# Starting two units of an output line beside the last attention tiles (second of three transformer blocks)

## The reference, cut to what matters

```
h = rmsnorm(x, attn_norm);  proj = h @ w_in
o_nsa  = head_rmsnorm(nsa_mixer(p_nsa),  nsa_out_gain)     # 6 heads of 64: features 0..383
o_rw   = rwkv7_mixer(p_rw)                                 # 4 heads of 64: features 384..639
o_moba = head_rmsnorm(moba_mixer(p_moba), moba_out_gain)   # 6 heads of 64: features 640..1023
x = x + concatenate([o_nsa, o_rw, o_moba]) @ w_out
x = x + conv_glu(rmsnorm(x, ffn_norm), ...)
```

## Time and profile before

| | us |
|---|---|
| median of three timed runs | 2748.77 |
| the three runs | 2742.35, 2748.77, 2754.93 |
| profiled execution, its own time | 2737.73 |
| its span, first to last instruction | 2735.6 |
| TensorE busy in it | 2610.8 (95%) |
| mean granted TensorE clock | 0.978 of full |

### The profile page before, as it was taken

The page is one execution under the profiler, slowest core; times in us unless marked ns, Lnnn a source line. Parts: engine busy times, 40 slices in busy tenths (PEclk is TensorE's granted clock), DMA queues, the critical chain, the costliest instruction groups (busy, mean ns, idle before and its releaser), DMA issues.

```text
span 2735.6 us, 35675 instructions
## 1 busy us (share of the span) xinstructions
PE 2610.8 (95%) x14346; PEld 2114.1 (77%) x14346; DVE 1514.5 (55%) x2530; ACT 1036.0 (38%) x1821; POOL 320.1 (12%) x263
## 2 busy tenths in 40 slices
PE   8989999999999999998989999999999999999998
PEld 6778888899998876766657777777766677788886
DVE  4787654554445456477646778454643544433444
ACT  3465444443223252235443223254333333322323
POOL 0043310012222010010002222020000000100001
PEclk9999999999999999998789999999999999999999
DMA  3211121223222331320024564232221122233332
GB/s 131 71 50 55 47 63 63 70 86 92 93 93 86 99 132 47 123 70 2 1 70 146 200 200 154 94 115 85 78 70 47 54 85 89 84 97 93 94 99 69
DMA packets 70849, 239.00 MB, mean 87 GB/s; under 512 B 12212, under 2 KB 13109, under 8 KB 70430
## 3 DMA queue, kind: packets, MB, share of 16 engines
q1 hardware_dynamic: 63342, 209.96, 24.3%
q10 hardware_dynamic: 7344, 26.77, 2.8%
HBM read 234.06 MB, written 2.64 MB: 87 GB/s over the span
## 4 chain that ended last, share of the span: by engine, by line
PE 64%; DVE 10%; ACT 4%; issue 2%; POOL 0%; ACTq 0%; DVEq 0%
PE ps L591 54%; DVE wl L375 2%; PE ps L2742 2%; ACT wh L363 1%; DVE arena L1060 1%; PE ps L3419 1%; DVE xl L672 1%; PE ps L1797 1%; PE ps L1781 1%; PE ps L1808 1%; DVE arena L3098 1%; PE ps L765 1%; PE ps L3405 1%; PE ps L1646 1%; DVE arena L1837 0%
## 5 line engine op out<-in xcount | busy, mean ns | idle before, releaser
L591 PE MATMUL ps<-xh,wh 128*128 128x512 f32 (+1 forms) x2728 | 1010.4, 385 | 27.6 <-DVE wl L375 8.2
L591 PE MATMUL ps<-xl,wh 128*128 128x512 f32 (+1 forms) x2728 | 991.1, 378 | 0.0
L591 PE MATMUL ps<-xh,wl 128*128 128x512 f32 (+1 forms) x2728 | 986.8, 376 | 0.0
L375 DVE TENSOR_TENSOR wl<-ring,wh 128x1024 fp32r<-128x1024 f32 x374 | 472.1, 1262 | 610.5 <-ACT wh L363 610.0
L363 ACT ACTIVATE wh<-ring 128x1024 fp32r<-128x1024 f32 x372 | 393.1, 1057 | 943.5 <-PE ps L591 841.9
L591 PEld LDWEIGHTS ps<-xh,wh 128*128 128x128 f32 x2728 | 501.3, 189 | 156.6 <-issue 43.1
L591 PEld LDWEIGHTS ps<-xh,wl 128*128 128x128 f32 x2728 | 501.4, 190 | 98.6
L591 PEld LDWEIGHTS ps<-xl,wh 128*128 128x128 f32 x2728 | 500.3, 189 | 97.5 <-issue 5.5
L2029 PE MATMUL ps<-xh,wh 128*128 128x264 f32 (+1 forms) x816 | 257.1, 315 | 5.5 <-DVE xl L429 5.3
L2029 PE MATMUL ps<-xl,wh 128*128 128x264 f32 (+1 forms) x816 | 232.0, 284 | 0.0
L2029 PE MATMUL ps<-xh,wl 128*128 128x264 f32 (+1 forms) x816 | 231.8, 284 | 0.0
(11 more groups left out here) (392 smaller groups left out, 2714.3 us busy)
## 6 DMA issues: line engine op xcount, KB each, us to landing
ring<-in_weights SPq DMA_DIRECT2D x374, 512.0 KB, 3.5
arena<-in_w_ada ACTq DMA_DIRECT2D x48, 512.0 KB, 4.5
arena<-in_cmp_w SPq DMA_DIRECT2D x2, 2048.0 KB
arena<-strip_scratch SPq DMA_DIRECT2D x8, 264.0 KB, 3.7
out_features<-arena SPq DMA_DIRECT2D x8, 256.0 KB, 2.1
h<-in_x ACTq DMA_DIRECT2D x2, 528.0 KB, 4.4
h<-in_x SPq DMA_DIRECT2D x2, 528.0 KB, 6.0
con<-in_consts SPq DMA_DIRECT2D x1, 777.0 KB, 10.0
```

The source lines that it names most:

```text
L375: dve.tensor_tensor(flat(self.wl[:, s % 2]), flat(self.ring[:, s % RING]), flat(self.wh[:, s % 2]).bitcast(F32), ALU.subtract).then_inc(se ...
L591: last = pe.matmul(self.place(u, e), w[:, k, :], x[:, k, o:o + m], start=(k == 0 and i == 0), stop=(k == self.chunks - 1 and i == 2))
```

## The change

- The last moba pair's tiles run in the order of row blocks 3, 2, 1, 0 (before: 0 to 3).
- Head norms 3 to 5 are due as soon as their pair is done, and use bank 7 as norms 0 to 2 do; the attention's users of bank 7 wait for them (tiles 17 and 21 are added to the list).
- The eight chunks are split in the order 0, 1, 2, 5, 6, 3, 4, 7, each with a due time of its own (`split`), the first seven among the attention's last steps; `rank` gives a chunk's place in that order for the waits.
- The first two units of the output line walk through a written list of 16 chunk steps (`early`): 0:0, 0:1, 0:2, 0:5, 1:0, 1:1, 1:2, 1:5, 0:6, 0:3, 0:4, 0:7, 1:6, 1:3, 1:4, 1:7 (unit:chunk), the first eleven due 0.2 apart from 1.05 before the line's begin. The line's begin moves from 1.3 after the last norm's due time to 0.35 before it.
- Its units take all eight banks in turn: 4, 5, 6, 7, 0, 1, 2, 3.

```diff
--- before.py
+++ after.py
@@ -517,7 +517,7 @@
         self.loads = range(core.issued, min(core.taken + RING, core.total))
         core.issued = max(core.issued, core.taken + RING)
         self.left = core.take("input_used", chunks - 1)
-        self.alone = None
+        self.alone, self.early = None, None
         core.chunk_used = [(self.left.sem, self.left.at(k + 1)) for k in range(chunks - 1)] + [(core.used, core.taken)] + core.chunk_used[chunks:]
 
     def pattern(self, u):
@@ -545,8 +545,11 @@
     def walk(self):
 
 
-        chunks, both = range(self.chunks), self.alone is not None
-        if both:
+
+        chunks, both = range(self.chunks), self.alone is not None or self.early is not None
+        if self.early:
+            yield from [(u, k) for _, u, k in self.early]
+        elif both:
             for k in chunks:
                 yield 0, k
                 if 0 <= k - self.alone < NC // 2:
@@ -556,7 +559,7 @@
 
     def planned_end(self, u):
 
-        return self.at + (u + 1) * self.d + (0.5 if self.alone is not None and u == 0 else 0)
+        return self.at + (u + 1) * self.d + (0.5 if (self.alone is not None or self.early) and u == 0 else 0)
 
     def place(self, u, e=0):
         _, m, b = self.pattern(u)[e]
@@ -579,13 +582,13 @@
         for n, (u, k) in enumerate(self.walk()):
             s = self.first + u
             wh, wl = core.wh[:, s % 2], core.wl[:, s % 2]
-            yield self.at + n / NC
+            yield self.early[n][0] if self.early and n < len(self.early) else self.at + n / NC
             if k == 0:
                 for sem, value in self.opened[u]:
                     pe.wait_ge(sem, value)
                 pe.wait_ge(core.split_done, s + 1)
             if u == 0 and self.inputs:
-                pe.wait_ge(self.inputs.lo.sem, self.inputs.lo.at(k + 1))
+                pe.wait_ge(self.inputs.lo.sem, self.inputs.lo.at(self.inputs.rank(k)))
             for i, (w, x) in enumerate(((wh, core.xh), (wh, core.xl), (wl, core.xh))):
                 for e, (o, m, _) in enumerate(self.pattern(u)):
                     last = pe.matmul(self.place(u, e), w[:, k, :], x[:, k, o:o + m], start=(k == 0 and i == 0),
@@ -651,10 +654,16 @@
         self.core, self.tiles, self.at, self.T, self.gains, self.ready = core, tiles, at, T, gains, ready
         self.free = core.chunk_used[0:len(tiles)]
         self.hi, self.lo = core.take("input_hi", len(tiles)), core.take("input_lo", len(tiles))
+        self.order = [(k, at + (k + 1) / NC + 0.02) for k in range(len(tiles))]
+
+    def rank(self, k):
+
+        return [j for j, _ in self.order].index(k) + 1
 
     def scalar(self, act):
-        for k, a in enumerate(self.tiles):
-            yield self.at + (k + 1) / NC + 0.02
+        for k, t in self.order:
+            a = self.tiles[k]
+            yield t
             if self.free[k]:
                 act.wait_ge(*self.free[k])
             if self.ready:
@@ -662,9 +671,10 @@
             act.activation(self.core.xh[:, k, 0:self.T], a, ACT.Copy, scale=self.gains[k] if self.gains else 1.0).then_inc(self.hi.sem, 1)
 
     def vector(self, dve):
-        for k, a in enumerate(self.tiles):
-            yield self.at + (k + 1) / NC + 0.14
-            dve.wait_ge(self.hi.sem, self.hi.at(k + 1))
+        for k, t in self.order:
+            a = self.tiles[k]
+            yield t + 0.12
+            dve.wait_ge(self.hi.sem, self.hi.at(self.rank(k)))
             xh, xl = self.core.xh[:, k, 0:self.T].bitcast(F32), self.core.xl[:, k, 0:self.T]
             if self.gains:
                 ins = dve.scalar_tensor_tensor(out=xl, in0=a, scalar=self.gains[k], in1=xh, op0=ALU.mult, op1=ALU.subtract)
@@ -682,6 +692,9 @@
         self.out = core.area(tmp, 2, SEQ)
         self.free = core.chunk_used[0:NC]
         self.made, self.hi, self.lo = core.take("normed", NC), core.take("input_hi", NC), core.take("input_lo", NC)
+
+    def rank(self, k):
+        return k + 1
 
     def scalar(self, act):
         for k in range(NC):
@@ -1766,7 +1779,7 @@
         t = self.tiles[s]
         if t >= 2:
             pe.wait_ge(self.out_used.sem, self.out_used.at(t - 1))
-        if t in (5, 9, 13):
+        if t in (5, 9, 13, 17, 21):
             pe.wait_ge(self.means.logs.sem, self.means.logs.at(t // 4))
 
     def tensor(self, pe):
@@ -1930,7 +1943,6 @@
 
 
 class HeadMeans(Stage):
-
 
 
     def __init__(self, core, items, sq, r):
@@ -3003,7 +3015,7 @@
                 t += widths[i]
         ends.append(t)
     for p in range(3):
-        for i in range(4):
+        for i in range(4) if p < 2 else (3, 2, 1, 0):
             steps.append(Causal(i, t, widths[i], P2[:, MQ + p], [P2[:, MK + p]] * 2, [half(2 + p, m) for m in range(2)]))
             t += widths[i]
         ends.append(t)
@@ -3033,25 +3045,19 @@
     items, free = [], 0
 
     def room(n):
-        def wait(pe):
-            if n < 3:
-                pe.wait_ge(attend.out_used.sem, attend.out_used.at(4 * n + 4))
-            elif n == 3:
-                pe.wait_ge(out.root.sem, out.root.at(2))
-        return wait
+        return lambda pe: pe.wait_ge(attend.out_used.sem, attend.out_used.at(4 * n + 4))
     for n in range(6):
         x = steps[8 * n + 7 if n < 3 else 24 + 4 * (n - 3) + 3]
-        free = max(free + 0.8, x.out + 0.02 if n < 3 else max(x.out + 0.1, scanned + 1.8))
-        items.append((free, x.q, core.p("nsa_out_gain_2" if n < 3 else "moba_out_gain_2", n % 3), attended(4 * n + 4), 7 if n < 3 else 5,
-                      room(n)))
+        free = max(free + 0.8, x.out + 0.02)
+        items.append((free, x.q, core.p("nsa_out_gain_2" if n < 3 else "moba_out_gain_2", n % 3), attended(4 * n + 4), 7, room(n)))
     means = HeadMeans(core, items, P2[:, NG], P2[:, MV + 2])
     attend.means = means
     out = RwkvOutput(core, scanned, scan, RO, bonus, G, tmp)
     later = [rwkv, tokens, compress, keys, inverse, fixed, cmp, scan, attend, out, means]
     for b, mine in ((0, (attend.masked.sem, attend.masked.at(72))), (1, (attend.masked.sem, attend.masked.at(72))),
                     (2, (attend.kept.sem, attend.kept.at(71))), (3, (attend.out_used.sem, attend.out_used.at(23))),
-                    (4, (out.root.sem, out.root.at(1))), (5, (means.root.sem, means.root.at(6))),
-                    (6, (attend.kept.sem, attend.kept.at(72))), (7, (attend.out_used.sem, attend.out_used.at(24)))):
+                    (4, (out.root.sem, out.root.at(1))), (5, (out.root.sem, out.root.at(2))),
+                    (6, (attend.kept.sem, attend.kept.at(72))), (7, (means.logs.sem, means.logs.at(6)))):
         core.drained[b] = mine
     Y = Q + [G[:, 0], G[:, 1]] + [P2[:, MQ + t] for t in range(3)]
 
@@ -3060,7 +3066,8 @@
             eng.wait_ge(out.done.sem, out.done.at(k - 2))
         else:
             means.ready(eng, k if k < 3 else k - 2)
-    return stages + lines + [Later(x, begin) for x in later], Y, ready, begin + free + 1.3
+    split = [(0, 42.6), (1, 42.75), (2, 42.9), (5, 43.05), (6, items[4][0] + 0.95), (3, 43.8), (4, 44.25), (7, free + 0.75)]
+    return stages + lines + [Later(x, begin) for x in later], Y, ready, begin + free - 0.35, [(k, begin + t) for k, t in split]
 
 
 class Convolved(Line):
@@ -3547,7 +3554,7 @@
             ahead[i] = next(both[i], None)
 
 
-def mixing_end_2(core, Y, ready, at):
+def mixing_end_2(core, Y, ready, at, split):
 
     T = SEQ
     h = [core.h_all[:, k, META:T1] for k in range(NC)]
@@ -3558,7 +3565,10 @@
     names = ("square_ready", "squares_added", "squares_summed", "root_ready")
     four = (0, 1, 2, 3)
     inputs = Inputs(core, Y, at - 1, T, ready=ready)
-    out = Added(core, at, WHOLE, (6, 7, 0, 1), inputs, NC, h)
+    inputs.order = split
+    out = Added(core, at, WHOLE, (4, 5, 6, 7, 0, 1, 2, 3), inputs, NC, h)
+    first = [(0, 0), (0, 1), (0, 2), (0, 5), (1, 0), (1, 1), (1, 2), (1, 5), (0, 6), (0, 3), (0, 4), (0, 7), (1, 6), (1, 3), (1, 4), (1, 7)]
+    out.early = [(at - 1.05 + 0.2 * n if n < 11 else at + n / NC, u, k) for n, (u, k) in enumerate(first)]
     sums = Sums(core, at, 1, h, out.ready, T, 4, tmp, r, names, late=True)
     stages = [inputs, out, sums]
     at += NC
```

## The result

Both kernels were timed 20 times on the same chip. Before: median 2742.75 us (2738.17 to 2754.93). After: 2749.06 us (2743.42 to 2754.01). The ratio is 1.002, with an interval of 1.0012 to 1.0029: the changed kernel is slower by some 6 us, 0.2%. That is inside the 0.5% that I called "same" and inside the range of 2733 to 2755, but it has the other sign than the 4.2 us of gain that I forecast.

A forecast was written before the change was run, and what follows sets the result against it. TensorE is 95% busy, so only its waits and slow clock at the attention-to-output seam could yield: 1417.4 - (1410.5 to 1414.9) - 0.5 = 2.0 to 6.4 us, taken as 4.2; 2748.8 - 4.2 = 2744.6 us, range 2733 to 2755.

The forecast's parts named there:

- (a): Head norm 3 moves behind pair 0's last tile, near 1353, beside the RWKV scan: cost 0 to 1.9 us, taken as 0.
- (b): Head norm 4 moves from behind the attention to behind pair 1: its chain leaves the tail, all of 4.13 us.
- (c): Seven chunk splits among the last attention tiles: 3.7 us on ScalarE, 4.3 on VectorE; TensorE waits 2.6, 1.3 and 2.2 us.
- (d): Eight triples of products between the last tiles, 5.6 to 10.2 us of TensorE work; three more under norm 5's chain.
- the walk: Instruction-by-instruction walk of three engine queues through the seam: unit 2 at 1410.5 to 1414.9 instead of 1417.4, before handoff cost.
- (e): Last pair from long tile to short: shorter chain in the last tile, but the long one sits where ScalarE is fullest.
- (f): New handoff to unit 2, whose weights can be split only into unit 0's buffer: adds 0.5 us (0 to 1).
- rival 1: Clock falls near 1386 in the gappier seam and the stream starts slow: gain 0 to 1 us, 2748.3; chance 0.20.
- my ceiling: TensorE idle time, slow products and slow attention steps in the seam: some 14 us (0.5% of the span) could go.
- Rival 2: Walk too gloomy; engines overlap better in the seam at high clock: gain 6.4 to 11 us, 2740; chance 0.17.
- Rival 3: Splits ahead of exponentials block ScalarE's queue; last tile another 3 us late, with low clock: slower, 2752; chance 0.10.
- Rival 4: Early chunk steps wait for their xl until the attention's end: only 4.1 us won, less 3, 2747.5; chance 0.08.

The follow-up runs named there:

- b_pad2: Kernel before with 2 extra wide products (0.46 us), result overwritten, in unit 4 of the second block's output line: 2755.02 us, ratio 1.004.
- b_late5: Kernel before with 5 extra products (1.16 us) in the third block's last output line, behind the narrow stretch: 2744.2 us, ratio 1.0.
- b_pad5: Kernel before with 5 extra wide products (1.16 us), result overwritten, in unit 4 of the second block's output line: 2756.87 us, ratio 1.0047.
- v2_pad3: Changed kernel with unit 2's wh made ahead of squaring unit 0's tile, plus 3 extra products (0.70 us) in the output line: 2746.03 us, ratio 1.0.
- a_before: Kernel before, unedited, timed again under another label: 2739.88 us, ratio 0.9997.
- a_after: Changed kernel, unedited, timed again: 2748.14 us, ratio 1.0018.
- e_reversed: Kernel before with only the last pair's tiles run from long to short: 2754.59 us, ratio 1.0038.
- a_forward: Changed kernel with the last pair's tiles from short to long again: 2748.45 us, ratio 1.0013.
- b_pad8: Kernel before with 8 extra wide products (1.85 us), result overwritten, in unit 4 of the second block's output line: 2756.52 us, ratio 1.0038.
- v2: Changed kernel with ScalarE making unit 2's wh ahead of squaring unit 0's tile: 2752.35 us, ratio 1.0021.
- e_norms: Kernel before with only head norms 3 to 5 due as soon as their pair is done, in bank 7: 2759.62 us, ratio 1.0061.
- a_pad13: Changed kernel with 13 extra wide products (3.01 us) in unit 4 of the second block's output line: 2743.45 us, ratio 1.0008.

## Why the prediction was wrong in sign

**The step that failed** is the sentence at the end of what bounds the kernel: "From there on both kernels run the same dense stream, so I compare only that time." They run the same instructions, but not at the same clock. The part of the sum that I left out is +6.3 us in the narrow stretch (and up to +2.1 behind it), against -3.07 that I compared. -3.07 + 6.3 to 8.4 is +3.2 to +5.3 us; the medians say +6.3 and +5.2. That the stretch is where it is lost is shown by its windows in fourteen profiles, that it depends on what is delayed ahead of it by b_pad2 and b_late5.

What orders the lengths is where in the 59 instructions the clock falls. Windows on both sides of the fall; before:

```profile
2010.92:2013.02 2.10, 2.10 (x9) 1.10 (x9) 1.17 (x2) 0.71 (x1) 0.00 (x0) 1.00 0.03 4
2013.03:2014.03 1.00, 1.00 (x3) 0.59 (x3) 0.00 (x0) 0.58 (x1) 0.00 (x0) 0.50 0.81 213
```

and b_pad5:

```profile
2017.72:2018.34 0.62, 0.62 (x5) 0.60 (x6) 0.62 (x1) 0.62 (x1) 0.00 (x0) 1.00 0.00 0
2018.35:2019.35 1.00, 1.00 (x3) 0.34 (x2) 0.54 (x2) 0.08 (x1) 0.00 (x0) 0.50 0.00 0
```

In the next table "delay" is the time from step 28 to the stretch, less the 659.79 us of before; "fall" is how long after the stretch's first product the granted clock falls.

| kernel | delay | fall | narrow stretch |
|---|---|---|---|
| v2_pad3 | -3.48 | 2.15 | 18.76 |
| before, a_before, b_late5 | 0, +0.03, +0.10 | 2.10, 2.08, 2.01 | 18.75, 18.77, 18.75 |
| after, a_after | -3.03, -3.04 | 1.71, 1.70 | 25.01, 25.04 |
| b_pad2, e_reversed | +0.50, +0.59 | 1.64, 1.56 | 28.15, 28.18 |
| a_forward, b_pad8 | -5.55, +1.39 | 0.86, 0.76 | 28.15, 28.15 |
| v2, e_norms, b_pad5 | -5.36, +1.45, +1.49 | 0.69, 0.67, 0.62 | 29.71, 29.70, 29.69 |
| a_pad13 | -0.10 | 1.20 before it | 22.84 |

Among the kernels that reach the stretch later than before does (by 0.03 to 1.49 us), each delay brings the fall forward by just as much, counted by instructions (to 0.05 us), and the stretch gets longer in steps (18.8, 28.2 and 29.7 us). The first of these steps is the one that b_pad2 meets. For the kernels that come 3 to 6 us sooner the delay alone does not give the place of the fall, nor for a_pad13, which finds the clock low already and has 3.81 us of idle time just ahead of the stretch where the others have 2.2 to 2.3. Why the clock falls at that moment is not shown. The kernel before meets the stretch well: of the ten changed kernels whose edit stands ahead of it, one (v2_pad3) met it as well and nine lost 4 to 11 us there. I had no chance for that among my rivals.

The Trainium skill, "TensorE: Matmul & The Clock Gate", section "A second HAM failure mode: psum-queue depth-cycling", speaks of frequent short idle times that make the clock swing. I weighed it for the seam only. The narrow stretch has no idle time at all after its first product, so a rule on idle times between groups says nothing on its 6.3 us. The trace has a swing there without them: in the kernel after the clock rises again and falls a second time 18.77 us into the stretch, where TensorE has not paused since its start:

```profile
2037.63:2038.63 1.00, 1.00 (x4) 0.80 (x3) 1.00 (x1) 0.28 (x1) 0.00 (x0) 0.50 0.00 0
```

Whether the 2.26 us of idle time just ahead of the stretch have a part in the first fall is open, as no kernel here goes without them.

**The seam, point by point.** Times are put on the clock of the kernel before by taking off 10.96 us. The timeline of TensorE of the kernel after, from the last two tiles on:

```profile
1391.50 1.10 PE L1980 MATMUL ps<-arena,con 128*128 128x512 f32 x2 [1.69 <-ACT arena L1964]
...
1399.66 0.91 PE L1810 MATMUL ps<-con,arena 128*128 128x128 f32 x3 [2.40 <-DVE arena L1861]
...
1402.57 0.78 PE L594 MATMUL ps<-xh,wh 128*128 128x512 f32 x1
...
1413.86 0.44 PE L1821 MATMUL ps<-arena 128*64 128x128 f32 x4
...
1415.43 1.10 PE L1980 MATMUL ps<-arena,con 128*128 128x512 f32 x2 [0.23 <-ACT arena L1964]
...
1420.21 0.50 PE L594 MATMUL ps<-xh,wh 128*128 128x512 f32 x1 [1.58 <-DVE xl L682]
...
1424.92 0.47 PE L594 MATMUL ps<-xh,wh 128*128 128x512 f32 x1 [0.97 <-DVE wl L375]
```

(a) Head norm 3 runs at 1354.84 on the old clock, where I put it. No run has this part alone, so its 0 is not tested.

(b) Norm 4's product is at 1391.50, two tiles before the end, and only norm 5's (1415.43) is behind the last weighted sum. That order is right, the worth is not: I took all 4.13 us for gain, and with (a) but without (c) and (d) it makes the seam 1.03 us longer, since the wait moves one tile forward. That it pays with (d), because products then fill that wait, is my reading; no run has (d) without it.

(c) ScalarE is the full engine, as the walk had it. (My sum for it was off: 14.35 and seven xh of 0.53 make 18.1, not 17.5; it stays within the 17 to 19 that I went on with.) From 1390.04 it works without a gap until 1402.2; its timeline shows splits between the exponentials:

```profile
1397.58 0.61 ACT L671 ACTIVATE xh<-arena 128x512 fp32r<-128x512 f32 x1
...
1398.25 0.60 ACT L1874 ACTIVATE arena<-arena 128x384 f32<-128x384 f32 x1
...
1398.85 0.62 ACT L671 ACTIVATE xh<-arena 128x512 fp32r<-128x512 f32 x1
1399.37 0.67 ACT L1924 ACTIVATE arena<-ps,con 128x512 f32<-128x512 f32 x1
1400.08 0.63 ACT L1925 ACTIVATE arena<-arena 128x512 f32<-128x512 f32 x1
1400.61 0.60 ACT L1874 ACTIVATE arena<-arena 128x384 f32<-128x384 f32 x1
...
1414.35 0.28 ACT L1889 ACTIVATE arena<-ps 128x128 f32<-128x128 f32 x1 [1.49 <-PE ps L1821]
```

TensorE's wait for tile 33's probabilities behind it is 2.40 us; I had 2.6. The 1.3 and 2.2 more that I had behind that came to 0.30, 0.88 and 0.36. The last tile's copy is at 1414.35, so at 1403.39 on the old clock, 8.81 us later than the earlier trace rows; I had 6.6 to 10.2. The sign that I named, over 85% busy from 1376 to 1392, is missed: 12.79 us of the 16 (80%).

(d) Eight triples run before norm 5's product and three behind it, in the order that I gave.

(e) I gave it no price of its own. It costs 2.29 us in the new order (a_forward) and 0.55 in the old one (e_reversed). I had said that the long tile would then sit where ScalarE is fullest; that this is the cause is likely and not shown.

(f) The handoff costs 1.12 us (v2), just beyond the upper end of my 0 to 1. ScalarE's timeline there:

```profile
1421.93 0.64 ACT L753 ACTIVATE arena<-h 128x512 f32<-128x512 f32 x1 [2.50 <-DVE h L859]
1422.47 1.04 ACT L363 ACTIVATE wh<-ring 128x1024 fp32r<-128x1024 f32 x1
```

I took the cost of the third block's handoff as 0.32 of idle time and 0.2 of pipeline; here 0.97 is idle. The square of unit 0's tile starts 0.54 us ahead of the wh, on which VectorE's wl and unit 2's first product wait in turn.

The seam's gain, then, is 3.07 us, within the 2.0 to 6.4 of the walk and 1.1 below the middle, 0.6 of that for (f).

**The clock in the seam (rival 1)** went neither way: between the first early product and norm 5's it is 0.86, and from 1415.43 on it is 1.00, so the stream does not start slow. Before, the first 12 products ran at 0.50. Windows of the kernel after:

```profile
1376.00:1394.86 18.86, 16.45 (x89) 9.59 (x88) 7.70 (x22) 9.06 (x22) 0.00 (x0) 0.74 0.00 0
...
1402.57:1415.43 12.86, 11.38 (x60) 7.22 (x59) 8.26 (x25) 5.94 (x19) 0.00 (x0) 0.86 0.00 1
1415.43:1424.92 9.49, 6.93 (x27) 4.73 (x27) 3.51 (x5) 4.39 (x6) 0.00 (x0) 1.00 0.00 0
```

The first window is partly slow (0.74). The kernel before had slow clock there too, and I had not looked: I read its clock from 1375.68 on, so my ceiling left out a slow stretch ahead of that, at 0.79 in all. (My 68% busy at the high clock is that of the whole window to 1394.86; up to 1390.62, where the clock is 1.00, it is 64%, 9.55 us of 14.94.) The second line here is the window 1376.00 to 1394.86 above, put on the old clock: 0.92 against 0.74.

```profile
1351.13:1375.68 24.55, 21.82 (x177) 14.79 (x176) 13.94 (x52) 9.07 (x30) 0.00 (x0) 0.79 0.00 1
1365.04:1383.90 18.86, 16.01 (x106) 8.75 (x104) 8.59 (x33) 12.10 (x36) 0.00 (x0) 0.92 0.00 0
```

Over the whole seam the new order has the higher clock all the same (0.85 against 0.81).

**Rival 2** (engines overlap better, over 6.4 us) did not come; a_forward's 5.36 comes near. **Rival 3** had the right sign with another cause: ScalarE's queue did block, at the cost that the walk had, and the time was lost 590 us later. **Rival 4** is refuted by the product at 1402.57, 12.86 us before norm 5's.

**The time** came out only 4.5 us from my 2744.6, and inside the range, by luck. I had put a gain of 4.2 on the median of three timings, 2748.77, and twenty timings put the kernel before at 2742.75: the base was 6.0 us too high and the change 10.5 us too good, and the two errors partly cancel. The rivals' own 2740 to 2752 hold the 2749.06, but for causes that did not come. The scatter of the timings goes by the same clock as the surprise: over the 32 executions of the kernel before that were timed beside the b_pads, the span goes from 2735.7 us at a mean clock of 0.978 to 2752.6 at 0.970, with a correlation of -0.97, some 1.8 us for each 0.001 of clock. I had used it as noise around a fixed difference.

## What to carry to other kernels

When an edit is worth a few microseconds in thousands, "the same instructions behind it" is not "the same time behind it": cut both profiles at common instructions and compare the parts, or the local gain and a clock effect far away are read as one number. Before judging a small edit by its median, run the kernel before with a useless half microsecond put in near the same place; if that alone moves the median by more than the edit should, as here (0.46 us, 12 us), the median judges the place in time, not the edit. And a step taken off the serial chain is not worth its length by itself: here the wait moved one tile forward, and the seam got longer.

## What the runs showed of the hardware that was not expected

- A stretch without idle time can run at either clock: the same 59 instructions of TensorE in the same order (a window can count one more at its edge) take 18.75 us at 0.91 or up to 29.7 us in other kernels. In b_pad2 they take 28.15 us at 0.58, with two more products some 580 us ahead as the only difference in TensorE's work. Here are b_pad2's windows over it:

```profile
2024.28:2052.43 28.15, 28.15 (x60) 14.82 (x60) 4.83 (x10) 6.20 (x11) 0.00 (x0) 0.58 0.12 38
```

- Time ahead of the change, in the same order of instructions, differs by up to 12.9 us from execution to execution (1351.13 against 1363.99) while ScalarE's busy time in these two agrees to 0.01 us. And yet the clock meets the seam alike: in all fourteen profiles it comes back to 2.4 GHz 0.2 to 0.3 us ahead of step 28. The windows from the start to the scores of step 28, of the kernel before:

```profile
0.00:1351.13 1351.13, 1280.84 (x8650) 1077.60 (x8650) 789.34 (x1547) 555.58 (x1141) 208.50 (x193) 0.98 0.23 75
```

and of b_pad2, whose added products come later:

```profile
0.00:1363.99 1363.99, 1295.51 (x8651) 1089.26 (x8651) 788.43 (x1547) 555.57 (x1141) 208.32 (x193) 0.96 0.23 74
```

- The waits of a seam bound by queues repeat far better than the kernel's total: 68.68, 68.67 and 68.69 us in three profiles of the changed order, 71.74 to 71.78 in six of the old one, while their spans range over 11.8 and 25.0 us (2740.1 to 2751.9, 2735.6 to 2760.6).
